# Adaptive-norm modulation of a two-layer diffusion trunk: fp32 products on the raw weights, spread over five places

## The reference, cut to what matters

```python
def ada_params(cond, w_mod, b_mod):
    m = jax.nn.silu(cond) @ w_mod + b_mod          # w_mod: 1024 x 6144, one per layer
    return jnp.split(m, 6, axis=-1)
...
    for layer in range(DEPTH):                     # DEPTH = 2
        hp = modulate(rms_norm(xp, norm1[layer]), mp[0], mp[1])   # x*(1+scale)+shift
        ...                                        # even: recurrence and pooling; odd: convolution and attention
        xp = xp + mp[2] * yp
        hp = modulate(rms_norm(xp, norm2[layer]), mp[3], mp[4])
        ...                                        # even: SwiGLU; odd: top-2 of 8 experts
        xp = xp + mp[5] * fp
```

## Time and profile before

| | |
|---|---|
| median of 3 runs | 2351.88 us (2350.11 to 2356.47) |
| the profiled execution | 2351.2 us, its span 2349.6 us |
| busy PE, DVE, ACT, POOL | 84%, 54%, 36%, 14% |
| chain that ended last | PE 67%, DVE 15%, issue 9% |
| mean granted TensorE clock | 0.892 |
| read from HBM | 262.86 MB, 122 GB/s over the span with what is written |

### The profile page before, as it was taken

The page is one execution under the profiler, slowest core; times in us unless marked ns, Lnnn a source line. Parts: engine busy times, 40 slices in busy tenths (PEclk is TensorE's granted clock), DMA queues, the critical chain, the costliest instruction groups (busy, mean ns, idle before and its releaser), DMA issues.

```text
span 2349.6 us, 35825 instructions
## 1 busy us (share of the span) xinstructions
PE 1967.4 (84%) x12234; PEld 1730.1 (74%) x12235; DVE 1257.9 (54%) x2029; ACT 856.9 (36%) x1348; POOL 327.8 (14%) x350
## 2 busy tenths in 40 slices
PE   4789486999999996898878886697978888896985
PEld 2489285999999983795333574697967888896983
DVE  4733764223323347315987547244866777865435
ACT  4722712222122237222223322243644655553321
POOL 2030202000000000205960003002101011101011
PEclk9979787999999999698577897798989998998996
DMA  9902011324621249222000021246867699866433
GB/s 286 313 21 73 18 37 45 108 78 128 161 80 42 74 143 329 76 72 54 3 0 0 1 78 63 65 119 184 231 178 213 181 254 260 237 191 169 122 90 134
DMA packets 439521, 288.47 MB, mean 123 GB/s; under 512 B 20890, under 2 KB 428666, under 8 KB 439332
## 3 DMA queue, kind: packets, MB, share of 16 engines
q1 hardware_dynamic: 425124, 248.75, 36.6%
q0 software_dynamic: 13024, 37.12, 5.3%
q10 hardware_dynamic: 1184, 0.51, 0.1%
HBM read 262.86 MB, written 23.47 MB: 122 GB/s over the span
## 4 chain that ended last, share of the span: by engine, by line
PE 67%; DVE 15%; issue 9%; ACT 3%; SPq 2%; DMA 2%; POOL 1%; ACTq 1%; DVEq 0%; POOLq 0%
PE ps L983 14%; PE ps L984 14%; PE ps L985 14%; PE ps L988 11%; PE ps L989 4%; DVE vp L1824 2%; PE ps L1051 2%; SPq L464 2%; DVE lo L1555 2%; PE ps L1269 1%; PE ps L1286 1%; ACT hi L613 1%; POOL tmp L2208 1%; DVE am L1885 1%; DVE h_both L1646 1%
## 5 line engine op out<-in xcount | busy, mean ns | idle before, releaser
L1555 DVE TENSOR_TENSOR lo<-raw,hi 128x1024 fp32r<-128x1024 f32 (+3 forms) x538 | 566.6, 1081 | 200.6 <-ACT hi L613 195.7
L613 ACT ACTIVATE hi<-raw 128x1024 fp32r<-128x1024 f32 (+3 forms) x538 | 495.6, 942 | 403.5 <-PE ps L985 255.9
L983 PE MATMUL ps<-h_both,hi 128*128 128x320 f32 x1728 | 546.8, 316 | 62.4 <-DVE h_both L1646 30.4
L984 PE MATMUL ps<-h_both,hi 128*128 128x320 f32 x1728 | 541.7, 313 | 0.0
L985 PE MATMUL ps<-h_both,lo 128*128 128x320 f32 x1728 | 541.6, 313 | 0.0
L983 PEld LDWEIGHTS ps<-h_both,hi 128*128 128x128 f32 x1728 | 330.8, 191 | 72.7 <-issue 41.0
L988 PE MATMUL ps<-h_both,hi 128*128 128x256 f32 (+2 forms) x1056 | 295.6, 367 | 60.8 <-issue 52.0
L984 PEld LDWEIGHTS ps<-h_both,hi 128*128 128x128 f32 x1728 | 331.6, 192 | 0.2 <-issue 0.2
L985 PEld LDWEIGHTS ps<-h_both,lo 128*128 128x128 f32 x1728 | 331.2, 192 | 0.0
L988 PEld LDWEIGHTS ps<-h_both,hi 128*128 128x128 f32 x1056 | 211.7, 200 | 70.3 <-issue 53.2
L989 PE MATMUL ps<-h_both,lo 128*128 128x128 f32 (+2 forms) x1056 | 257.6, 244 | 0.0
(11 more groups left out here) (324 smaller groups left out, 2617.3 us busy)
## 6 DMA issues: line engine op xcount, KB each, us to landing
raw<-in_moe_w_dram SPq DMA_DIRECT2D x160, 512.0 KB, 5.2
raw<-in_w_mod_dram SPq DMA_DIRECT2D x96, 512.0 KB, 7.7
raw<-in_moe_w_dram SPq DMA_DIRECT2D x64, 384.0 KB, 3.5
raw<-in_ff_w_dram SPq DMA_DIRECT2D x40, 512.0 KB, 4.9
raw<-in_moe_w_dram SPq DMA_DIRECT2D x64, 320.0 KB, 3.8
y_rows<-zeros POOLq DMA_DIRECT2D x22, 512.0 KB, 4.2
raw<-in_moe_w_dram SPq DMA_DIRECT2D x32, 256.0 KB, 2.9
raw<-in_ev_w_in_dram SPq DMA_DIRECT2D x12, 512.0 KB, 8.8
```

What stands on the lines that cost most here:

```text
L613: act.activation(hi[c % 2][:, parts[h]], raw[c % 4][:, parts[h]], ACT.Copy).then_inc(hi_done, 1)
L983: pe.matmul(out, w_hi, v_hi, start=first, stop=False, skip_group_check=True)
L984: pe.matmul(out, w_hi, v_lo, start=False, stop=False, skip_group_check=True)
L1555: dve.tensor_tensor(lo[c % 2][:, parts[h]], raw[c % 4][:, parts[h]], hi[c % 2][:, parts[h]].bitcast(F32), ALU.subtract).then_inc(lo_done, 1)
```

## The change

- **Products.** A modulation chunk is no longer split. PE multiplies the raw fp32 weights as the moving operand with the two fp32 columns `cs` standing: 8 products of 2 x 256 in place of 16. ACT and DVE have nothing to do for it but one row copy, and the ring buffer is freed by PE (`mod_done`).
- **Places.** The 48 chunks are spread: 4 at the start, 2 behind the turning of x, 2 behind the sums of norm 0; 12 in the recurrence, its gates numbered 0 to 7 (4 behind gate 3, one behind each of gates 5 and 6, 3 behind gate 7, one and two around the last pooling products); 8 behind the sums of norm 1; 2 ahead of and 2 behind the sums of norm 2, and 4 more before the gemm; 1 ahead of the rotary stage, 5 between its steps and 2 behind it; 4 behind the sums of norm 3.
- **Rows.** `mrow` keeps two rows. Each is turned at once by two transposes into the upper half of its bank (`fold`), after the next chunk's products (in the rotary stage, where all chunks use one bank, ahead of them). ACT copies a row between its other work (`mod_row`), from the second norm on after every second tile k (`with_k`), and a finished group to `mod` (`mod_keep`).
- **Waits.** PE waits for `mod_kept` ahead of each stage that reuses those banks, so ahead of the gemms behind norms 0, 1 and 2. The first two chunks of EIN and of MOE are now split behind their norm's root and behind norm 3, no longer ahead.
- The gates of the context share a bank, `swap` uses one bank in place of two, and ACT, DVE and SP write the two halves of the SwiGLU out instead of looping.

```diff
+MODS = [(0, 8, 0), (8, 12, EOUT + 2), (20, 8, FF + 2), (28, 8, OIN + 2), (36, 8, OOUT + 2), (44, 4, MOE)]
+KEPT = [(0, 8), (8, 12), (20, 4), (24, 4), (28, 4), (32, 4), (36, 8), (44, 4)]
...
-            def mod_chunk(slot, n):
-                wh = hi[slot][:, :].rearrange("p (k c) -> p k c", k=KT)
-                wl = lo[slot][:, :].rearrange("p (k c) -> p k c", k=KT)
+            def fold():
+
+                q = waiting.pop()
+                pe.wait_ge(mod_rows, q + 1)
+                for i in range(2):
+                    at = 256 + 2 * (q % N_MOD * 2 + i)
+                    last = pe.transpose(ps[:, mod_bank(q), at:at + 2], mrow[:, q % 2, i * P:(i + 1) * P], ident[0:2, 0:2])
+                last.then_inc(mod_folded, 1)
+
+            def mod_chunk(q):
+
+                r = ring_of_mod(q)
+                w = raw[r % 4][:, :].rearrange("p (k c) -> p k c", k=KT)
                 for k in range(KT):
...
+                    if k % (KT // 2) == 0:
+                        pe.wait_ge(slot_in[r % 4][k // (KT // 2)], 16 * landed(r))
+                    if k == 0 and q >= 2:
+                        pe.wait_ge(mod_rows, q if mod_bank(q) == 7 else q - 1)
+                    last = pe.matmul(ps[0:2, mod_bank(q), 0:256], cs[:, k, :], w[:, k, :], start=k == 0, stop=k == KT - 1, skip_group_check=True)
+                last.then_inc(mod_done, 1)
...
-            with pe.Fori(0, N_MOD // 2) as pr:
-                for u in range(2):
-                    begin(M1 + 2 * pr + u)
-                    mod_chunk(u, M1 + 2 * pr + u)
+            mods(28, 2)
             pe.wait_ge(evac, 2 * OIN)
             norm_pe(2)
-            fold(mrow1)
+            mods(30, 2, True)
+            pe.wait_ge(mod_kept, 5)
+            mods(32, 4, True)
+            pe.wait_ge(mod_kept, 6)
...
             for i in range(5):
                 spread(i)
+                mods(37 + i, 1)
                 if i >= 1:
                     swap(i - 1)
 
             swap(4)
             pe.transpose(ps[:, 5, 2 * P:3 * P], kf[:, 0:P], ident).then_inc(v_turned, 1)
+            mods(42, 2, True)
...
+            def first_weights():
+                mod_row(6, 2)
+                mod_keep(0)
+                split_hi(EIN)
+                split_hi(EIN + 1)
+
+            norm_act(0, lambda k: (x_kept, 10), first=first_weights)
...
-            norm_act(1, lambda k: (evac, 2 * (EOUT + k // 2 + 1)))
+            norm_act(1, lambda k: (evac, 2 * (EOUT + k // 2 + 1)), first=lambda: mod_row(20), with_k=lambda c: mod_row(21 + c))
+            mod_row(25, 3)
+            mod_keep(2)
+            mod_keep(3)
```

More of the change, by code:

```diff
@@ L49, with ring_of, ring_of_mod, landed @@
 N_ITEM = N_UP + KT
[L50 to L57, removed]
+EIN, EOUT, FF, OIN, OOUT, MOE = 0, 6, 10, 50, 57, 61
+MODS = [(0, 8, 0), (8, 12, EOUT + 2), (20, 8, FF + 2), (28, 8, OIN + 2), (36, 8, OOUT + 2), (44, 4, MOE)]
+KEPT = [(0, 8), (8, 12), (20, 4), (24, 4), (28, 4), (32, 4), (36, 8), (44, 4)]
+X_BANKS = (4, 6, 7)
+def ring_of(n):
+    return n + sum(count for _, count, before in MODS if before <= n)
+def ring_of_mod(q):
+    return q + [before for first, _, before in MODS if first <= q][-1]
+MANY = [(ring_of(OIN + c), 3) for c in range(2)] + [(ring_of(OOUT + c), 1) for c in range(4)]
+def landed(r):
+    return r // 4 + 1 + sum(more for m, more in MANY if m <= r and m % 4 == r % 4)
+def taken_before(r):
+    for q in range(2 * N_MOD):
+        if ring_of_mod(q) == r - 4:
+            return "mod", q
+    for n in range(MOE):
+        if ring_of(n) == r - 4:
+            return "weight", n
 JH = 6
@@ L505, in _ @@
[L505 to L515, removed]
@@ L626, in mod_fours @@
[L626 to L632, removed]
+            act.activation(cs[:, :, 0], par[:, 1, CX:CX + KT], ACT.Silu)
+            act.activation(cs[:, :, 1], par[:, 1, CS:CS + KT], ACT.Silu).then_inc(cs_silu, 1)
+            act.wait_ge(ab_lam, 1)
@@ L850, in _ @@
             for c in range(4):
-                split_hi(OOUT + c + 2)
-            norm_act(3, lambda k: (evac, 2 * (OOUT + k // 2 + 1)), hf)
+                if c < 2:
+                    split_hi(OOUT + c + 2)
+            norm_act(3, lambda k: (evac, 2 * (OOUT + k // 2 + 1)), hf, with_k=lambda c: mod_row(44 + c))
+            mod_keep(7)
+            for c in range(2):
+                split_hi(MOE + c)
             act.wait_ge(r_mm, 1)
@@ L1641, in norm_dve @@
                 t_of(1)
+                if first is not None:
+                    first()
                 for k in range(KT):
-                    if k == 3 and layer is not None:
-                        mod_params(layer, 1)
                     dve.wait_ge(n_hi, KT * i + k + 1)
@@ L1648, in norm_dve, with first_weights @@
                         t_of(k + 2)
-            norm_dve(0, layer=0)
+            def first_weights():
+                mod_params(0, part=0)
+                split_lo(EIN)
+                split_lo(EIN + 1)
+            norm_dve(0, first=first_weights)
             for c in range(2):
@@ L1932, in _ @@
             ln_lo(NC - 1)
+            mod_params(6, part=1)
             for c in range(4):
                 residual_pair(c % 2, OOUT + c, c, 1)
-                split_lo(OOUT + c + 2)
+                if c < 2:
+                    split_lo(OOUT + c + 2)
             norm_dve(3, hf)
+            mod_params(7)
+            for c in range(2):
+                split_lo(MOE + c)
             dve.wait_ge(r_turned, 1)
```

371 lines of the change are left out of this document (209 added, 162 removed).

## The result

The changed kernel takes **2264.0 us** (median of 4 runs, 2256.4 to 2267.0); the kernel before took 2351.0 (median of 4, 2347.6 to 2356.5). The ratio is 0.962, 95% interval 0.959 to 0.965. The prediction was 2268. The profiled run took 2263.0 us, its span is 2261.4, its granted clock 0.919.

| stretch | predicted | measured |
|---|---|---|
| start, to the first gemm that runs freely | -49 | -49.9 |
| EIN gemm | 0 | +0.5 |
| recurrence, to the end of the EOUT gemm | +2 | +4.1 |
| norm 1, with its sums, to the SwiGLU | +11 | +11.6 |
| norm 2, SwiGLU's end to OIN's end | -69 | -69.8 |

The account below looks back on a forecast made before the run. The first stage was taken as bound by bringing 24 MB of modulation weights, DVE close behind. Terms -49 + 2 + 11 - 69 + 16 + 6 = -83 on 2351.2 us gave 2268 us; 8-in-10 range 2250 to 2306.

Parts of the forecast that it names:

- Start: Start to first free gemm: fewer chunks ahead, DMA no limit any more, tile 0's `lo` at 86.7 us, not 135.7: -49 us.
- Recurrence: Recurrence: twelve chunks partly fill PE's idle time; output gemm starts later but warm: +2 us (0 to 8).
- Norm 1: Norm 1: eight chunks and waits for row copies start the gemm some 10 us late and lose its tile run: +11 us.
- Norm 2: Norm 2: 24 chunks fewer ahead, eight around it; SwiGLU's end to gemm 49.6 less 2, against 117.1 us: -69 us.
- Rotary: Rotary stage: eight chunks where PE is on the chain, at a warm clock, delay attention: +16 us.
- Rival 1: Rotary stage stays at 1.2 GHz: +54 in place of +16, total 2306 us; chance 0.16, alone or in part.
- Norm 3: Norm 3: four chunks hidden behind the tiles, but the last row copy and fold delay the router's products: +6 us.
- The gemms and experts at nothing: Gemms not touched, written-out SwiGLU loops costed at nothing, experts and the end predicted at 0.
- (2): Everywhere: fp32 products with two columns never lift the clock: +97, total 2448 us; chance 0.05.
- (3): Some 20 exposed chunks: waits between chunk, row and fold cost one more microsecond each, total 2288 us; chance 0.16.
- (4): Less is lost: folds at 0.2, recurrence and norm 3 cover all, total 2256 us; chance 0.60 together with the forecast.

Follow-up runs that it names:

- e7: Changed kernel with the splits of EIN's first weight ahead of norm 0's variance and DVE's split of the second behind tile 7: 2255.3 us.
- e12: Changed kernel with one product in place of eight in each of the recurrence's twelve chunks: that stage 256.8 us, from 264.2; total of another routing.
- e1: Changed kernel with all 24 chunks of layer 0 ahead of its first norm, none in the recurrence, four left in norm 1: 2314.3 us.
- e3: Changed kernel with one product in place of eight in each of norm 1's eight chunks: norm 1 28.1 us, from 33.0; total 2387.7 us, other routing.
- e6: Changed kernel with ACT's row copies earlier among the tiles of norms 1 and 2: 2249.4 us.
- e2: Changed kernel with one product in place of eight in each rotary chunk: rotary stage 33.9 us, from 48.0; total 2344.4 us, other routing.
- e4: Changed kernel with the eight rotary chunks moved into attention, two products behind each of four steps of a head: 2243.8 us.
- e5: e4 with norm 3's four chunks in attention too, the first four heads taking two chunks each, four products a step: 2255.9 us.
- e10: Changed kernel with norm 3's row copies alone earlier: 2259.2 us.
- e11: e5 with the splits of the first two expert weights ahead of norm 3 again: 2256.4 us, one run.
- e8: Changed kernel with 64 further two-column fp32 products added in attention, nothing moved or removed: 2262.3 us.
- e9: Changed kernel with the edits of e4, e6 and e7 together, and norm 3's row copies earlier too: 2235.2 us.

## Why the prediction was right, point by point

**Start (-49; measured -49.9).** Right, with two errors that cancel. Norm 0's reciprocal starts 57.2 us earlier, not some 54: the folds took 0.21 to 0.29 us where I took 0.4, turning x 6.5 where I took 8, so the sums began at 60.4 where I had 63, and they took 8.88. Behind it the way to the free gemm is 7.2 us longer (31.2 for 24.0). I counted 4.9 for DVE's splits and not what they do to POOL; e7 got 5.6 of the 7.2 back.

**Recurrence (+2; +4.1).** The mechanism was right, the size off, inside the 0 to 8. DVE's last step came 2.8 us late, counted from EIN's end, and the last gate 2.2. I had let the pause of 3 us pass at a warm clock; the chunk behind it took 5.19 us. From EIN's end to the end of the EOUT gemm are 133.7 us against 129.6 before; with one product a chunk (e12) it is 128.3, with no chunk (e1) 128.4. So the term is products in line; the copies' waits cost nothing once these are gone. Whether earlier copies would have paid too, as in norm 1, was not run. My own sum ends at 325.1 (311 + 14.1), not at the 326.4 that it names; the term is within its range either way.

**Norm 1 (+11; +11.6).** Right, with one term missing and one cost that did not show. From the end of the sums the gemm starts 9.9 us later (35.4 for 25.5), where I had 10. The lost run along the tiles (3.1) and the warm clock (2.7) cancel: the SwiGLU behind it kept its length. The other 1.7 us are the sums, 10.5 us for 8.9, which I took as unchanged; in e1, without any chunk ahead of them in this stage, they took 10.5 too, and in e12 8.9, so it is not the chunks alone that decide it. In the stage itself e3 takes 3.4 us back at the SwiGLU's end by leaving products out and e6 3.9 by moving copies alone; they overlap, so neither is a share.

**Norm 2 (-69; -69.8).** Right, and for the reason given: the gemm starts 44.3 us behind the SwiGLU where I had 46.5, against 117.1 before, and without its run along the tiles it takes 2.9 us longer (100.9 for 98.0). It still held 5.4 us that a better order of copies recovers (e6).

**Rotary (+16; +15.5).** Right. Spreads and swaps at about half their time pay for part of the eight chunks: e2 and e4 give 14.1 and 13.8 us back, and with the chunks moved away (e4, e5) it takes 34.2 and 32.8 us, like the 32.6 before, at 0.59 in e4. Rival 1, a stage that stays at 1.2 GHz, did not happen: 0.96 from 990 to 1038 us. By the rule of the Trainium skill, "TensorE: Matmul & The Clock Gate", Part 1, that I weighed there, PE's own activity releases the throttle, and this stretch agrees; that the span 1100 to 1121 us of the kernel before, busy throughout, did not rise no run here explains.

**Norm 3 (+6; +5.7).** Right by itself (e10). What failed is that I costed the moved splits of MOE 0 and 1 only where they went. They had stood ahead of the norm's squares, and taking them away there gave 3.1 us (70.35 for 67.21, e11).

**The gemms and experts at nothing.** The SwiGLU kept its time (464.9 us for 464.8). Behind the router's copy the profile shows -3.5 us; kernels here with the same expert code and the same routing had 906.8 to 919.7 us in one profile each, so this is not told apart from chance.

**Rivals.** (2), no lift of the clock by two-column products, is refuted by 3.54 us a chunk and by e8. (3), waits between chunk, row and fold, was there: e6 and e10 take back 3.9, 5.4 and 5.9 us. I had put about that much into the terms, so it is no extra. (4), less is lost, came half true: the folds took 0.21 to 0.29 us, but the recurrence and norm 3 did not cover their chunks. That the total lies between (4) and the sum is in part luck: the 3.2 us of the moved splits and the 3.5 behind the router's copy stood in no term.

**Open.** Attention. Kernels that do not touch it had 192.5 to 198.2 us in nine profiles, and the same interleaved code had 191.5 (e4, clock 0.87) and 205.6 (e9, 0.80). e5, with up to four products a step, had 213.3 and e11, the same there, 213.4. Four a step cost more than two; how much of the 21.8 us is the place of the clock's steps and how much the products was not separated. The traces narrow it. From a head's first score to the next head's, e4 has 20.5, 20.4 and 20.6 us in its fifth, sixth and seventh head, all at a granted clock of 1.00; e9, with the same code, has 24.8 at 0.79, 20.4 at 1.00 and 23.9 at 0.86, and its third head takes 29.1 at 0.77 for 23.8 at 0.93. e5 takes 23.9 at 0.86 in its seventh head, which holds the products of e4's. So kernels with equal work differ where the clock is lower; what sets it there no run shows.

## What to carry to other kernels

Ask of a block of work not what it costs but who waits for it: the same fp32 chunks, dearer for PE, gained 50 and 70 us where they left a place at which every engine waited, and cost 14 to 15 where PE itself was on the chain. Work that is threaded through a stage brings small copies on a third engine; where these stand in its queue was worth 15 us here (e6, e10) and is cheap to try. And when work is moved, cost the place that it leaves as well as the one it goes to.

## What the runs showed of the hardware

- fp32 products with two columns of weights and 256 moving columns take 0.44 us each at the full clock (3.54 us for eight, 9.25 for the first sixteen from a cold start), and they raise the clock: 0.70 to 0.83 in attention by 64 of them, at no gain in time.
- A stage of equal instructions can take 191.5 or 205.6 us (attention in e4 and e9), at a granted clock of 0.87 or 0.80; heads at 1.00 took 20.4 to 20.6 us, the same heads at 0.79 and 0.86 took 24.8 and 23.9.
- A POOL piece of 512 columns took 3.83 us beside DVE's subtractions and 0.77 without.
- Leaving out modulation products changed the experts' part by 96 to 132 us through the routing; such kernels can be compared only stage by stage.
